# Vector-engine intermediates of a two-part transformer kernel move from SBUF tiles to PSUM banks

## Chip, cores and metric

The kernel runs on one core of one Trainium2 chip. The metric is the device time of one execution in microseconds; the number to predict is the median of several runs.

## What is computed

A 512-token sequence of width 1024 goes through a first block (two layers of feed-forward, mixer, feed-forward and a gated side input) and a second block (four more mixers). What the change touches, in the reference's words:

```python
def swiglu(x, w_in, w_out):
    a, b = jnp.split(x @ w_in, 2, axis=-1)
    return (jax.nn.silu(a) * b) @ w_out

def conformer_conv(glu_in, conv_w, conv_b, g_conv):          # in the mixer of both layers
    a = glu_in[..., :CONV_CH] * jax.nn.sigmoid(glu_in[..., CONV_CH:])
    y = lax.conv_general_dilated(a, conv_w[:, None, :], ..., feature_group_count=CONV_CH) + conv_b
    return jax.nn.silu(rmsnorm(y, g_conv))                    # 31 taps, 512 channels

def hybrid_mixer(u, ...):
    y_attn = forgetting_attention(q, k, v, f_logit) @ w_attn_out   # 8 heads of 64
    y_conv = conformer_conv(z[..., C0:GA0], ...) @ w_conv_out
    merged = jax.nn.sigmoid(z[..., GA0:GC0]) * y_attn + jax.nn.sigmoid(z[..., GC0:]) * y_conv
    return merged @ w_out

def s5_branch(...):                                           # second block
    y = s5_mixer(...); y = y * jax.nn.sigmoid(y @ w_glu + b_glu)
    return (y * jax.nn.silu(z)) @ w_out
```

## The kernel before

All activations are held transposed: 128 channels on the partitions, 512 tokens along the row. A large product is a `Gemm`: one output tile of 128 channels by 512 tokens accumulates in PSUM bank 0 or 1, in turn. Every operand is split into a high part and a low part, and a tile of K = 1024 takes 24 matmuls: high weight times high and low activation for each of 8 chunks (lines 326 and 327), then low weight times high activation (line 335). ScalarE copies the weight's high part out of the DMA buffer (`WH`, line 286), GpSimd subtracts to get the low part (`WL`, line 264, about 2.4 us), and SyncE loads the next weights when `WL` is done. VectorE reads the finished bank (which frees it for the tile after the next) and prepares what follows. When the result is itself an operand of a later product, `split` (lines 407 and 410) makes its halves: a cast into the high tile, then a subtraction into the low tile.

PSUM has eight banks: 0 and 1 for the products' tiles, 2 and 3 for attention scores, 4 and 5 for transposes, 6 and 7 for head values (bank 7 also for the sum of squares at the stage borders).

The places that the change touches:

- **Feed-forward** (`b_vec`, lines 1667 to 1671): the gate product goes through the SBUF tiles `T` and `T2` and is then split into `HH` and `HL`. 88 such tiles.
- **Convolution** (`Conv`, lines 1754 to 1796): 15 of 31 taps per channel group run on VectorE as `y = y + w*x` in the SBUF tile `Y` (line 1763, 176 instructions), the other 16 are multiplied on ScalarE (line 1786) into a ring of four tiles and summed on GpSimd (`YP`, line 1796). `close` (line 1774 and the two after it) adds the two sums. All of this is woven into the products of V, of Q and K, and of the 16 gate tiles (`G`, line 1901): after each product tile every engine's program does its share of the thread. The order is fixed in program text.
- **Attention of the mixer** (`Heads`): also woven into the gate tiles. Pairs of heads go through steps s = 0, 1, ...; PE writes scores of step s, transposes of step s-2 and values (line 1091) of step s-3. VectorE takes maxima (line 1105) and scales (line 1118), and copies a finished pair of heads out of its bank (line 1893) four steps behind. Values of even pairs are in bank 6, of odd pairs in bank 7; PE waits for the copy of the pair before the last.
- **Merging** (`conv_part`, lines 1977 to 1980): eight tiles of K = 512, each with four VectorE instructions: product, sum, cast, subtraction. The product with `w_out` then reads `MH`, `ML`.
- **Gating in the S5 branch** (`glu`, lines 2830 to 2833), **side input** (`flip_p`) and **gated heads** of the second block (`gated_heads`).

The names: `T`, `T2`, `FUN`, `PRE`, `Y`, `YP`, `CA` (convolution input), `G` (gates), `UF`, `ZG`, `PV` (a table of per-channel constants, used as a pointer scalar) are SBUF tiles; `ps` is PSUM.

Of the kernel before, what the change touches and what calls it, by code (L numbers as in the profile page):

```python
# [8 lines left out]
F32 = mybir.dt.float32  # L9
# [3 lines left out]
ALU = mybir.AluOpType  # L13
# [3 lines left out]
P = 128  # L17
# [21 lines left out]
TC = 8  # L39
# [79 lines left out]
class Machine:  # L119


    def __init__(self, nc, ctx):
# [40 lines left out]
        self.ps = ctx.enter_context(nc.psum_tensor("ps", [P, 8, SEQ], F32))  # L163

# [861 lines left out]
class Heads(Thread):  # L1026
# [16 lines left out]

    def block(self, x):

        s, p = divmod(x, 2)
        return 2 * (s // TT) + p, s % TT
# [17 lines left out]
    def tensor(self, e):  # L1065
# [4 lines left out]
        for s in range(self.pairs + lag + 1):  # L1070
# [11 lines left out]
            if s >= lag + 1:  # L1082
                a = 2 * (s - lag - 1)
                e.wait_ge(m.turned.sem, self.b + a + 2)
                h, n = self.block(a)
                if n == 0 and self.h0 + h // 2 > 1:
                    e.wait_ge(m.head_out.sem, self.h0 + h // 2 - 1)
                nb = self.blocks(n)
                for j in range(nb):
                    for p in range(2):  # L1090
                        mm = e.matmul(m.ps[HD * p:HD * p + HD, 6 + h // 2 % 2, n * P:(n + 1) * P], self.v(h + p, n, j),  # L1091
                                      self.buf.PT[:, p, j * P:(j + 1) * P], start=(j == 0), stop=(j == nb - 1))
                        if j == nb - 1:
                            mm.then_inc(m.valued.sem, 1)
# [29 lines left out]
    def heads_out(self, e, s):  # L1124

        m = self.m
        if s < 0 or s % TT != TT - 1:
            return
        c = s // TT
        e.wait_ge(m.valued.sem, self.b + 2 * s + 2)  # L1130
        self.freed = (m.head_out.sem, self.h0 + c + 1)
        self.out(self, e, c, m.ps[:, 6 + c % 2, :])
# [33 lines left out]
    frees = Gemm.frees  # L1166

# [158 lines left out]
def build(nc, out, a):  # L1326
    with ExitStack() as ctx:
# [330 lines left out]
        def ffn(l, w_in, w_out, next_gain, beside, kind=Gemm):  # L1658
# [3 lines left out]
            def pair_of_tiles(first):  # L1662
                tiles = []
                for p in range(2):
                    def b_vec(g, e, i, ps, p=p):
                        v = m.vec
                        e.tensor_tensor(m.T[:], ps, m.R[:], ALU.mult).then_inc(*g.frees())  # L1667
                        e.wait_ge(m.act_out.sem, g.a)
                        e.wait_ge(*v.last)
                        e.tensor_tensor(m.T2[:], m.T[:], m.FUN[:, (g.a0 + p) % 2, :], ALU.mult).then_inc(*v.next())  # L1670
                        g.split(e, at(HH, i * 2 + (first * 2 + p)), at(HL, i * 2 + (first * 2 + p)), m.T2[:])
# [26 lines left out]
        def mixer(l):  # L1698
# [46 lines left out]
            class Conv(Thread):  # L1745
# [7 lines left out]
                def vector(self, e):  # L1753
                    for i in range(CC):
                        y = Y[:, i, :]
                        for j in range(DVE_TAPS):
# [5 lines left out]
                            else:  # L1762
                                e.scalar_tensor_tensor(y, src, wj, y, ALU.mult, ALU.add).then_inc(*v.next())  # L1763
# [130 lines left out]
            att = Heads(m, B, HEADS, q=lambda h, n: head(0, h, slice(n * P, (n + 1) * P)),  # L1894
# [111 lines left out]
        def ple(l):  # L2006
# [5 lines left out]
            def flip_p(c):  # L2012
# [588 lines left out]
        def s5():  # L2601
# [223 lines left out]
            def glu(c):  # L2825
                def f(g, e, i, ps):
# [3 lines left out]
                    e.tensor_tensor(times_(m.T2[:]), UF[:, c, :].rearrange("p (s c) -> p c s", s=TC), times_(ZG[:, c, :]), ALU.mult).then_inc(*v.next())  # L2830
# [50 lines left out]
        def gated_heads(z, high, low):  # L2881

            def f(g, e, c, ps):
                e.wait_ge(*v.last)
                e.tensor_tensor(m.T[:], ps, z[:, c, :], ALU.mult).then_inc(*v.next())
                e.wait_ge(*v.last)
                e.tensor_copy(high[:, c, :], m.T[:]).then_inc(*v.next())
                e.wait_ge(*v.last)
                e.tensor_tensor(low[:, c, :], m.T[:], high[:, c, :].bitcast(F32), ALU.subtract).then_inc(*g.frees())
# [529 lines left out]
```

## Time and profile before

| | us |
|---|---|
| median of 3 runs | 3542.94 (3540.14 to 3543.17) |
| the profiled execution | 3545.91, of which the span 3544.1 |
| TensorE busy in it | 3366.8 (95%) |
| VectorE busy | 2109.5 (60%) |
| GpSimd busy | 1428.6 (40%) |
| ScalarE busy | 1130.3 (32%) |
| mean granted TensorE clock | 0.973 |

The profile gives, for each instruction group, the line of the kernel, the engine, the tiles written and read and its durations. A busy TensorE says little by itself: what counts is whether a product tile takes its shortest period, or longer because a bank was not free or an operand not ready. So the chain that ended last and the waits in order of time are read stage by stage.

### The profile page before, as it was taken

How to read it: one execution, taken by the hardware profiler on the slowest of the kernel's cores; microseconds unless marked ns; L12 is line 12 of the kernel's file. 1: busy time of each engine (PE TensorE's matmuls, PEld its weight loads, DVE VectorE, ACT ScalarE, POOL GpSimd, SP SyncE). 2: the span in 40 equal slices, each digit the busy share in tenths (PEclk: the TensorE clock that was granted, in tenths of full speed). 3: DMA queues.
4: the chain of work that ended last, by engine and by line, in shares of the span. 5: the costliest groups of instructions: out<-in, count | busy, mean ns of one | idle time of the engine just before them, and what ended most of it. 6: DMA issues, size and time to landing. Idle time of an engine off the chain costs nothing.

```text
span 3544.1 us, 43859 instructions
## 1 busy us (share of the span) xinstructions
PE 3366.8 (95%) x16266; PEld 2635.9 (74%) x16266; DVE 2109.5 (60%) x2930; ACT 1130.3 (32%) x1846; POOL 1428.6 (40%) x693
## 2 busy tenths in 40 slices
PE   9999999899999999999998999998989988998998
PEld 6888777678887688887666788876776666776776
DVE  6743399787633576426987864336554648475653
ACT  3222234422222322223343222223324642343332
POOL 4444464344444344445453444443242223322341
PEclk9999999899999999999998999999999989999999
DMA  5333332144423344333212343344642212222221
GB/s 137 95 114 91 95 90 57 45 122 128 134 85 99 95 124 142 91 98 90 71 45 80 116 141 90 94 149 113 211 114 64 60 44 68 60 48 60 85 84 48
DMA packets 632187, 335.01 MB, mean 95 GB/s; under 512 B 97773, under 2 KB 621678, under 8 KB 630478
## 3 DMA queue, kind: packets, MB, share of 16 engines
q1 hardware_dynamic: 607006, 285.75, 28.8%
q10 hardware_dynamic: 23680, 44.32, 3.4%
q0 software_dynamic: 1328, 2.62, 0.2%
q8 instruction: 110, 1.80, 0.2%
q14 instruction: 63, 0.52, 0.0%
HBM read 308.65 MB, written 23.98 MB: 94 GB/s over the span
## 4 chain that ended last, share of the span: by engine, by line
PE 81%; DVE 13%; ACT 3%; issue 2%; ACTq 0%; POOL 0%; DVEq 0%
PE ps L335 24%; PE ps L326 24%; PE ps L327 23%; DVE Y L1763 3%; PE ps L1091 2%; PE ps L1056 1%; PE ps L1080 1%; PE ps L496 1%; DVE T L2832 1%; DVE UL L815 1%; DVE T L824 1%; DVE X L829 0%; PE ps L3204 0%; DVE SS L428 0%; DVE NM L1105 0%
## 5 line engine op out<-in xcount | busy, mean ns | idle before, releaser
L264 POOL TENSOR_TENSOR WL<-RAW,WH 128x1024 fp32r<-128x1024 f32 (+4 forms) x606 | 1321.1, 2182 | 2071.5 <-ACT WH L286 2071.4
L326 PE MATMUL ps<-UH,WH 128*128 128x512 f32 x3056 | 1233.4, 404 | 72.3 <-DVE UL L815 24.8
L327 PE MATMUL ps<-UL,WH 128*128 128x512 f32 x3056 | 1204.6, 394 | 0.0
L286 ACT ACTIVATE WH<-RAW 128x1024 fp32r<-128x1024 f32 (+4 forms) x605 | 571.0, 945 | 1199.8 <-PE ps L335 1169.3
L335 PE MATMUL ps<-UH,WL 128*128 128x512 f32 x3056 | 767.7, 392 | 4.5 <-POOL WL L264 4.5
L326 PEld LDWEIGHTS ps<-UH,WH 128*128 128x128 f32 x3056 | 580.4, 190 | 240.7 <-issue 47.0
L327 PEld LDWEIGHTS ps<-UL,WH 128*128 128x128 f32 x3056 | 580.5, 190 | 125.6 <-issue 7.0
L335 PEld LDWEIGHTS ps<-UH,WL 128*128 128x128 f32 x3056 | 570.9, 188 | 134.3 <-issue 8.6
L326 PE MATMUL ps<-HH,WH 128*128 128x512 f32 x704 | 279.2, 397 | 0.0
L327 PE MATMUL ps<-HL,WH 128*128 128x512 f32 x704 | 276.9, 393 | 0.0
L1763 DVE SCALAR_TENSOR_TENSOR Y<-CA,PV,Y 128x512 f32<-128x512 f32 x176 | 244.8, 1391 | 6.4
L1667 DVE TENSOR_TENSOR T<-ps,R 128x512 f32<-128x512 f32 x88 | 60.8, 691 | 303.3 <-PE ps L335 303.3
L434 DVE SCALAR_TENSOR_TENSOR X<-ps,X 128x512 f32 x48 | 33.2, 692 | 334.5 <-PE ps L335 334.5
L407 DVE CAST HH<-T 128x512 fp32r<-128x512 f32 (+1 forms) x88 | 198.7, 2258 | 5.9 <-DVE T L1670 3.2
L364 DVE TENSOR_TENSOR PRE<-ps,R 128x512 f32<-128x512 f32 x144 | 99.2, 689 | 172.8 <-PE ps L335 168.4
L1676 ACT ACTIVATE FUN<-PRE 128x512 f32<-128x512 f32 x88 | 55.6, 632 | 446.0 <-DVE PRE L364 446.0
L335 PE MATMUL ps<-HH,WL 128*128 128x512 f32 x704 | 185.0, 395 | 0.0
L326 PEld LDWEIGHTS ps<-HH,WH 128*128 128x128 f32 x704 | 132.1, 188 | 33.4
L335 PEld LDWEIGHTS ps<-HH,WL 128*128 128x128 f32 x704 | 132.1, 188 | 32.1
L327 PEld LDWEIGHTS ps<-HL,WH 128*128 128x128 f32 x704 | 132.1, 188 | 30.8
L1148 ACT ACTIVATE S<-ps,NM 128x128 f32<-128x128 f32 (+3 forms) x128 | 66.3, 524 | 126.3 <-DVE NM L1105 121.4
L1080 PE MATMUL ps<-IDENT,S 128*128 128x128 f32 x432 | 72.0, 298 | 23.1 <-ACT PT L1163 11.0
(434 smaller groups left out, 3565.9 us busy)
## 6 DMA issues: line engine op xcount, KB each, us to landing
RAW<-w_ff_in SPq DMA_DIRECT2D x176, 512.0 KB, 3.8
RAW<-w_in SPq DMA_DIRECT2D x72, 512.0 KB, 3.8
RAW<-w_ff_out SPq DMA_DIRECT2D x64, 384.0 KB, 3.4
RAW<-w_ff_out SPq DMA_DIRECT2D x64, 320.0 KB, 3.1
RAW<-d_w_in SPq DMA_DIRECT2D x24, 512.0 KB, 3.8
CM<-cm_dram ACTq DMA_DIRECT2D x8, 1088.0 KB, 10.6
RAW<-b_w_in SPq DMA_DIRECT2D x17, 512.0 KB, 3.7
RAW<-w_out SPq DMA_DIRECT2D x16, 512.0 KB, 3.9
```

The costliest lines, as they stand in the source:

```text
L264: e.tensor_tensor(m.WL[:, s, 0:k, :], m.RAW[:, r, 0:k, :], m.WH[:, s, 0:k, :].bitcast(F32), ALU.subtract).then_inc(m.low_ready.sem, 1)
L286: e.activation(m.WH[:, s, 0:k, :], m.RAW[:, r, 0:k, :], ACT.Copy).then_inc(m.high_ready.sem, 1)
L326: e.matmul(out, m.WH[:, s, c, 0:t.cols], H[:, k0 + c, :], start=(x == 0 and c == 0), stop=False)
L327: e.matmul(out, m.WH[:, s, c, 0:t.cols], L[:, k0 + c, :], start=False, stop=False)
L335: mm = e.matmul(out, m.WL[:, s, c, 0:t.cols], H[:, k0 + c, :], start=False, stop=last)
L364: ins = t.pre(e, i, pre, ps) if t.pre else e.tensor_tensor(pre, ps, m.R[0:t.cols, :], ALU.mult)
L407: e.tensor_copy(high, src).then_inc(*v.next())
L1080: mm = e.transpose(m.ps[:, 4 + a % 2, j * P:(j + 1) * P], self.buf.S[:, a % 4, j * P:(j + 1) * P], m.IDENT[:])
L1091: mm = e.matmul(m.ps[HD * p:HD * p + HD, 6 + h // 2 % 2, n * P:(n + 1) * P], self.v(h + p, n, j), self.buf.PT[:, p, j * P:(j + 1) * P], st ...
L1148: e.activation(B.S[:, c, 0:kk], m.ps[:, 2 + x % 2, 0:kk], ACT.Exp, bias=B.NM[:, c:c + 1], accum_out=B.RS[:, c:c + 1]).then_inc(m.exped.sem, 1)
L1667: e.tensor_tensor(m.T[:], ps, m.R[:], ALU.mult).then_inc(*g.frees())
L1763: e.scalar_tensor_tensor(y, src, wj, y, ALU.mult, ALU.add).then_inc(*v.next())
```

## The change

- `WORK` is PSUM bank 7. The products that are split into halves (feed-forward, merging, S5 gating) are made in place in `WORK` and not in `T`, `T2`; cast and subtraction read it there. `b_vec` gets a wait on VectorE's own last instruction ahead of its first write. In `gated_heads` the values' own bank is used.
- The 15 VectorE taps run in bank 7; the last tap writes `Y` in SBUF.
- Since bank 7 is taken, the mixer's attention uses `OneBankHeads`: all pairs' values are in bank 6, PE waits for the copy of the pair just before, and the copy of a finished pair (but for the last) stands one step earlier in VectorE's program.
- The side input's halves are made straight from its transposed bank, without the copy to `T`; the bank is released after the second instruction.

```diff
+        self.WORK = self.ps[:, 7, :]
...
+class OneBankHeads(Heads):
+    def value_bank(self, c):
+        return 6
+    def wait_values_left(self, e, h, n):
+        if n == 0 and self.h0 + h // 2 > 0:
+            e.wait_ge(self.m.head_out.sem, self.h0 + h // 2)
+    def heads_out(self, e, s):
+        if (s + 1) // TT < self.pairs // TT - 1:
+            s += 1
+        elif s // TT < self.pairs // TT - 1:
+            return
+        super().heads_out(e, s)
...
                     def b_vec(g, e, i, ps, p=p):
-                        e.tensor_tensor(m.T[:], ps, m.R[:], ALU.mult).then_inc(*g.frees())
+                        e.wait_ge(*v.last)
+                        e.tensor_tensor(m.WORK, ps, m.R[:], ALU.mult).then_inc(*g.frees())
...
-                        e.tensor_tensor(m.T2[:], m.T[:], m.FUN[:, (g.a0 + p) % 2, :], ALU.mult).then_inc(*v.next())
-                        g.split(e, at(HH, ...), at(HL, ...), m.T2[:])
+                        e.tensor_tensor(m.WORK, m.WORK, m.FUN[:, (g.a0 + p) % 2, :], ALU.mult).then_inc(*v.next())
+                        g.split(e, at(HH, ...), at(HL, ...), m.WORK)
...
-                        y = Y[:, i, :]
+                        y = m.ps[:, 7, :]
...
-                                e.scalar_tensor_tensor(y, src, wj, y, ALU.mult, ALU.add).then_inc(*v.next())
+                                dst = Y[:, i, :] if j == DVE_TAPS - 1 else y
+                                e.scalar_tensor_tensor(dst, src, wj, y, ALU.mult, ALU.add).then_inc(*v.next())
...
-                    e.tensor_tensor(m.T2[:], ps, G[:, DC + c, :], ALU.mult).then_inc(*g.frees())
+                    e.tensor_tensor(m.WORK, ps, G[:, DC + c, :], ALU.mult).then_inc(*g.frees())
                     e.wait_ge(*v.last)
-                    e.tensor_tensor(m.T2[:], G[:, c, :], m.T2[:], ALU.add).then_inc(*v.next())
-                    g.split(e, MH[:, c, :], ML[:, c, :], m.T2[:])
+                    e.tensor_tensor(m.WORK, G[:, c, :], m.WORK, ALU.add).then_inc(*v.next())
+                    g.split(e, MH[:, c, :], ML[:, c, :], m.WORK)
...
-                    e.tensor_copy(m.T[:], bank).then_inc(*g.frees())
-                    g.split(e, PH[:, c, :], PL[:, c, :], m.T[:])
+                    e.tensor_copy(PH[:, c, :], bank).then_inc(*v.next())
+                    e.wait_ge(*v.last)
+                    e.tensor_tensor(PL[:, c, :], bank, PH[:, c, :].bitcast(F32), ALU.subtract).then_inc(*v.next())
...
-                    e.tensor_tensor(m.T2[:], m.T2[:], g.fun, ALU.mult).then_inc(*v.next())
-                    g.split(e, M2H[:, c, :], M2L[:, c, :], m.T2[:])
+                    e.tensor_tensor(m.WORK, m.WORK, g.fun, ALU.mult).then_inc(*v.next())
+                    g.split(e, M2H[:, c, :], M2L[:, c, :], m.WORK)
```

The instructions of TensorE, ScalarE, GpSimd and SyncE keep their order. On VectorE, in the woven attention of the first layer, before the change (`S` is a scaled block of probabilities, `QKV` takes the heads' values, `NM` a maximum):

```order
L1118 TENSOR_SCALAR S<-S,RINV 128x256 x2
L1901 TENSOR_TENSOR G<-ps,R 128x512
L1763 SCALAR_TENSOR_TENSOR Y<-CA,PV,Y 128x512 x4
L1105 TENSOR_REDUCE NM<-ps 128x1 x2
L1112 RECIPROCAL RINV<-RSUM 128x1 x2
L1118 TENSOR_SCALAR S<-S,RINV 128x384 x2
L1893 COPY QKV<-ps 128x512
L1901 TENSOR_TENSOR G<-ps,R 128x512
```

The same place of VectorE's program after the change:

```order
L1125 TENSOR_SCALAR S<-S,RINV 128x256 x2
L1922 COPY QKV<-ps 128x512
L1930 TENSOR_TENSOR G<-ps,R 128x512
L1792 SCALAR_TENSOR_TENSOR ps<-CA,PV,ps 128x512 x4
L1112 TENSOR_REDUCE NM<-ps 128x1 x2
```

The copy of the pair's values has moved ahead of one gate tile's read-out, four taps and one step of attention; the taps read and write `ps`.

On VectorE in the merging stage, one tile before the change:

```order
L1977 TENSOR_TENSOR T<-ps,G 128x512
L1979 TENSOR_TENSOR T<-G,T 128x512
L407 CAST MH<-T 128x512
L410 TENSOR_TENSOR ML<-T,MH 128x512
```

And after it:

```order
L2006 TENSOR_TENSOR ps<-ps,G 128x512
L2008 TENSOR_TENSOR ps<-G,ps 128x512
L408 CAST MH<-ps 128x512
L411 TENSOR_TENSOR ML<-ps,MH 128x512
```

The count and the order of the four are the same; each now has one operand in PSUM.

## Rows read from the trace of the kernel before

**Rows 1.** The page: busy times, the chain that ended last, the taps' group.

```profile
PE 3366.8 (95%) x16266; PEld 2635.9 (74%) x16266; DVE 2109.5 (60%) x2930; ACT 1130.3 (32%) x1846; POOL 1428.6 (40%) x693
...
PE 81%; DVE 13%; ACT 3%; issue 2%; ACTq 0%; POOL 0%; DVEq 0%
...
L1763 DVE SCALAR_TENSOR_TENSOR Y<-CA,PV,Y 128x512 f32<-128x512 f32 x176 | 244.8, 1391 | 6.4
```

**Rows 2.** Stretches: bounds, length, busy us (instructions) of PE, PEld, DVE, ACT, POOL, clock, DMA.

```profile
187.74:242.14 54.40, 54.40 (x241) 45.05 (x240) 25.99 (x25) 13.22 (x15) 24.82 (x10) 1.00 0.42 132
...
471.31:518.05 46.74, 42.63 (x185) 34.02 (x184) 45.20 (x44) 16.86 (x20) 27.96 (x14) 0.96 0.33 90
518.05:647.69 129.64, 122.10 (x678) 90.98 (x679) 116.63 (x169) 51.41 (x120) 64.52 (x31) 0.97 0.20 53
...
697.89:732.39 34.50, 30.03 (x121) 23.38 (x120) 28.35 (x34) 6.54 (x9) 15.35 (x9) 0.95 0.42 122
2577.58:2628.69 51.11, 42.52 (x171) 32.66 (x170) 40.66 (x38) 12.55 (x16) 16.73 (x7) 0.91 0.42 122
```

**Rows 3.** VectorE by line: count, duration in ns min/median/max, first and last start.

```profile
L1763 DVE SCALAR_TENSOR_TENSOR Y<-CA,PV,Y x176: 750/752/2958, 445.6 to 1853.0; 128x512 f32<-128x512 f32 x176
...
L407 DVE CAST HH<-T x88: 426/2504/2515, 39.9 to 2222.4; 128x512 fp32r<-128x512 f32 x64, 128x512 f32 x24
...
L1667 DVE TENSOR_TENSOR T<-ps,R x88: 676/692/692, 38.4 to 2220.9; 128x512 f32<-128x512 f32 x88
...
L2832 DVE TENSOR_TENSOR T<-T,FUN x8: 2716/2798/2857, 2573.7 to 2620.2; 128x512 f32<-128x512 f32 x8
...
L1893 DVE COPY QKV<-ps x8: 679/682/692, 584.8 to 1867.2; 128x512 f32<-128x512 f32 x8
```

**Rows 4.** Timeline, Q/K and first gate tile: start, length, engine, line, [idle before].

```profile
509.24 2.93 DVE L1763 SCALAR_TENSOR_TENSOR Y<-CA,PV,Y 128x512 f32<-128x512 f32 x2
...
509.26 0.50 PE L326 MATMUL ps<-UH,WH 128*128 128x512 f32 x1 [2.06 <-DVE QKV L1808]
...
516.47 0.60 PE L1832 MATMUL ps<-IDENT,QKV 128*128 128x128 f32 x4
...
526.12 0.49 PE L1056 MATMUL ps<-QKV 64*128 64x128 f32 x4 [2.33 <-DVE V L1878]
```

**Rows 5.** Timeline, the gate tiles of the first layer.

```profile
552.82 0.73 ACT L1786 ACTIVATE T<-CA,PV 128x512 f32<-128x512 f32 x1 [4.19 <-POOL YP L1796]
...
555.47 0.49 PE L1056 MATMUL ps<-QKV 64*128 64x128 f32 x4 [1.82 <-ACT S L1148]
...
619.15 2.70 DVE L1774 TENSOR_TENSOR Y<-Y,YP 128x512 f32<-128x512 f32 x1
...
625.37 0.83 PE L1056 MATMUL ps<-QKV 64*128 64x256 f32 x4 [2.45 <-ACT S L1148]
```

**Rows 6.** Timeline, merging stage of the first layer: first and last VectorE instruction, PE's wait.

```profile
700.96 0.69 DVE L1977 TENSOR_TENSOR T<-ps,G 128x512 f32<-128x512 f32 x1 [1.92 <-issue]
...
729.22 0.69 DVE L410 TENSOR_TENSOR ML<-T,MH 128x512 fp32r<-128x512 f32 x1
...
729.97 0.50 PE L326 MATMUL ps<-MH,WH 128*128 128x512 f32 x1 [1.00 <-DVE ML L410]
```

**Rows 7.** Timeline, S5 gating: one VectorE period and PE's wait behind the last.

```profile
2604.71 0.74 DVE L2875 TENSOR_SCALAR PRE<-ps,PV 128x512 f32<-128x512 f32 x1
2606.16 1.05 DVE L2830 TENSOR_TENSOR T<-UF,ZG 128x512 f32<-128x512 f32 x1 [0.70 <-ACT FUN L2874]
...
2611.21 0.74 DVE L2875 TENSOR_SCALAR PRE<-ps,PV 128x512 f32<-128x512 f32 x1
...
2624.26 0.79 PE L326 MATMUL ps<-M2H,WH 128*128 128x512 f32 x1 [5.69 <-DVE M2L L410]
```

**Rows 8.** Timeline: values of a pair's last step, and VectorE's attention step that goes with it.

```profile
636.73 1.09 PE L1091 MATMUL ps<-PT,V 128*64 128x128 f32 x16
...
638.40 1.01 DVE L1105 TENSOR_REDUCE NM<-ps 128x1 f32<-128x384 f32 x2
```

More of the change, by code:

```diff
@@ L1042, in __init__ @@
         self.t0 = m.tiles
+    def value_bank(self, c):
+        return 6 + c % 2
+    def wait_values_left(self, e, h, n):
+        if n == 0 and self.h0 + h // 2 > 1:
+            e.wait_ge(self.m.head_out.sem, self.h0 + h // 2 - 1)
     def block(self, x):
@@ L1085, in tensor @@
                 h, n = self.block(a)
-                if n == 0 and self.h0 + h // 2 > 1:
-                    e.wait_ge(m.head_out.sem, self.h0 + h // 2 - 1)
+                self.wait_values_left(e, h, n)
                 nb = self.blocks(n)
@@ L1090, in tensor @@
                     for p in range(2):
-                        mm = e.matmul(m.ps[HD * p:HD * p + HD, 6 + h // 2 % 2, n * P:(n + 1) * P], self.v(h + p, n, j),
+                        mm = e.matmul(m.ps[HD * p:HD * p + HD, self.value_bank(h // 2), n * P:(n + 1) * P], self.v(h + p, n, j),
                                       self.buf.PT[:, p, j * P:(j + 1) * P], start=(j == 0), stop=(j == nb - 1))
@@ L1131, in heads_out @@
         self.freed = (m.head_out.sem, self.h0 + c + 1)
-        self.out(self, e, c, m.ps[:, 6 + c % 2, :])
+        self.out(self, e, c, m.ps[:, self.value_bank(c), :])
     def values(self, e, h, n, x):
@@ L1666, in b_vec @@
                         v = m.vec
-                        e.tensor_tensor(m.T[:], ps, m.R[:], ALU.mult).then_inc(*g.frees())
+                        e.wait_ge(*v.last)
+                        e.tensor_tensor(m.WORK, ps, m.R[:], ALU.mult).then_inc(*g.frees())
                         e.wait_ge(m.act_out.sem, g.a)
                         e.wait_ge(*v.last)
-                        e.tensor_tensor(m.T2[:], m.T[:], m.FUN[:, (g.a0 + p) % 2, :], ALU.mult).then_inc(*v.next())
-                        g.split(e, at(HH, i * 2 + (first * 2 + p)), at(HL, i * 2 + (first * 2 + p)), m.T2[:])
+                        e.tensor_tensor(m.WORK, m.WORK, m.FUN[:, (g.a0 + p) % 2, :], ALU.mult).then_inc(*v.next())
+                        g.split(e, at(HH, i * 2 + (first * 2 + p)), at(HL, i * 2 + (first * 2 + p)), m.WORK)
                     for half in range(2):
@@ L1893, in out_heads @@
                 e.tensor_copy(QKV[:, 2 * CC + c, :], ps).then_inc(*g.frees())
-            att = Heads(m, B, HEADS, q=lambda h, n: head(0, h, slice(n * P, (n + 1) * P)),
+            att = OneBankHeads(m, B, HEADS, q=lambda h, n: head(0, h, slice(n * P, (n + 1) * P)),
                         k=lambda h, n: head(CC, h, slice(0, (n + 1) * P)),
@@ L2020, in vec @@
                     e.wait_ge(*v.last)
-                    e.tensor_copy(m.T[:], bank).then_inc(*g.frees())
-                    g.split(e, PH[:, c, :], PL[:, c, :], m.T[:])
+                    e.tensor_copy(PH[:, c, :], bank).then_inc(*v.next())
+                    e.wait_ge(*v.last)
+                    g.si += 1
+                    e.tensor_tensor(PL[:, c, :], bank, PH[:, c, :].bitcast(F32), ALU.subtract).then_inc(*v.next())
+                    e.wait_ge(*v.last)
+                    e.sem_inc(m.splits.sem, 1)
+                    e.sem_inc(*g.frees())
+                    v.last = m.splits.sem, g.s0 + g.si
                 return pe, vec
@@ L2884, in f @@
                 e.wait_ge(*v.last)
-                e.tensor_tensor(m.T[:], ps, z[:, c, :], ALU.mult).then_inc(*v.next())
+                e.tensor_tensor(ps, ps, z[:, c, :], ALU.mult).then_inc(*v.next())
                 e.wait_ge(*v.last)
-                e.tensor_copy(high[:, c, :], m.T[:]).then_inc(*v.next())
+                e.tensor_copy(high[:, c, :], ps).then_inc(*v.next())
                 e.wait_ge(*v.last)
-                e.tensor_tensor(low[:, c, :], m.T[:], high[:, c, :].bitcast(F32), ALU.subtract).then_inc(*g.frees())
+                e.tensor_tensor(low[:, c, :], ps, high[:, c, :].bitcast(F32), ALU.subtract).then_inc(*g.frees())
             return f
```

4 lines of the change are left out of this document (3 added, 1 removed).

## Prediction

> **What bounds the kernel now.** I first read the page's busy times and its chain. TensorE is busy 95% of the span and has 81% of the chain; VectorE has 13% of it [rows 1]. So a faster VectorE pays only where TensorE waits for it, and the next question is where a product tile takes longer than it must. In the feed-forward, ten tiles of K = 1024 take 54.40 us without an idle moment, 5.44 us each, with VectorE busy for half the time [rows 2]. That is the floor of a tile. The feed-forward has most of the tiles, so most of the kernel can't move.
>
> Then I compared other stretches with that floor. In the Q/K stretch (471 to 518) TensorE is busy 42.63 of 46.74 us and VectorE 45.20: VectorE is full there. The gate stretch (518 to 648), the merging (698 to 732) and the S5 gating (2578 to 2629) leave TensorE idle for 7.5, 4.5 and 8.6 us, at a mean clock of 0.97, 0.95 and 0.91 [rows 2]. The second layer repeats the first three.
>
> Last I asked why VectorE is full. Its durations split in two: a tap (line 1763) takes 0.752 us at the median and up to 2.958; the cast into `HH` 0.426 at least and 2.504 at the median; the gate product at line 2832 never less than 2.716; but line 1667, of the same size and with one operand in PSUM, 0.676 to 0.692 over all 88, and the copy out of PSUM at line 1893 0.679 to 0.692 [rows 3]. The long ones read and write SBUF only. They last until a GpSimd instruction ends: GpSimd holds something that VectorE then waits for, and operations with their tensor in PSUM don't need it. That is what the change uses.
>
> The Trainium skill says it so in "SBUF — State Buffer", section "Who interferes with whom": VectorE and GpSimd share a pair of SBUF ports as an exclusive lock, which a VectorE instruction wants with two SBUF inputs or in a two-port mode (cast and copy from SBUF to SBUF). This trace agrees by the durations above; whether a tap with `CA` and the pointer scalar in SBUF and only `y` in PSUM is free of it, no row here shows, and by that rule it is.
>
> **Part 1, feed-forward: 0.** 88 casts go from 2.5 to about 0.69, as line 1893 [rows 3]. VectorE loses some 88 x 1.8 = 160 us of busy time and no path is shorter, since TensorE never waits for it there [rows 2]. The new wait ahead of `b_vec` stands on VectorE's own last instruction, which is done. The cover is large: even doubled, four instructions are under 6 us in two tiles of 5.44.
>
> **Part 2, Q/K stretch: 6.8 us per layer.** Seven tiles take 46.74 us [rows 2]; seven floors are 38.1. Four of them carry a set of four transposes, each at most 0.60 us and, since 0.2 of that overlaps the matmul behind it, about 0.37 [rows 4]: 1.5 to 2.4 us. What is left is 6.3 to 7.2 us; I take 6.8. It consists of waits for a bank that VectorE reads late (2.06 us at 509.26, behind two taps that took 2.93 us together where 1.5 would do [rows 4]) and of the clock, which is at 0.96 of full over the stretch [rows 2]. With taps at 0.75, VectorE's work per tile (one read-out, about two taps, the decay preparation) falls from some 6.5 us to about 4, below 5.44, so a bank is read as soon as it is full and all of this goes.
>
> **Part 3, gate stretch: 6.4 us per layer.** TensorE idles 7.5 us and the clock (0.97 over 129.64 us) costs about 3.4 more [rows 2]. Each wait has another cause. The 2.33 us at 526.12 are for a copy of V that stands behind taps [rows 4]; it goes, and I estimate that half of the lost clock goes with it: 4.0. The 1.82 us at 555.47 are for ScalarE's exponential, but ScalarE was itself held 4.19 us by GpSimd's `YP` and got free at 552.82 [rows 5]. A faster tap only makes GpSimd a little earlier, as it too no longer waits: 1.1. A remainder of 0.9 (7.5 less the three waits named) sits behind four taps: 0.9. The 2.45 us at 625.37 come behind `close`, whose addition at 619.15 took 2.70 us with both tensors in SBUF [rows 5]; it is not changed: 0.4. Sum 6.4. The end of the stretch, from 648 to 666, waits for GpSimd's last sum and stays.
>
> The moved copy of head values: before, PE has written them by 637.8 (636.73 plus 1.09) and VectorE gets to the step at 638.40 [rows 8]. After, it gets there up to 3 us earlier, but its maxima of that step need scores that PE makes just ahead of those values, so it waits at most 1.1 us, three times a layer. Behind it are queued one read-out and the taps, with a tile of slack: 0. PE wants bank 6 again one tile later, some 6 us after the copy: 0.
>
> **Part 4, merging: 5.0 us per layer.** Eight tiles of four instructions run from 700.96 to 729.91, 3.62 us each, and the `w_out` product waits for the last `ML` until 729.97 [rows 6]. After, all four take 0.69 (as line 1667) plus gaps, 2.98: the cast that was 0.43 at best gets slower, those of up to 2.5 [rows 3] go. 8 x 2.98 = 23.9, so `ML` is ready at 724.9. This is still slower than TensorE's 2.72 (half of 5.44), so VectorE stays the bound here.
>
> By the Trainium skill, "VectorE: DVE Perf Modes", section "The TRN2 errata — SBUF-src ops pay a fixed extra latency per instruction", a read from PSUM has a fixed part of 120 cycles against 58, which I estimate at 0.065 us for each; the trace's 0.692 at line 1667, the same as the subtraction of 0.69 from SBUF [rows 3, 6], speaks against it.
>
> **Part 5, S5 gating: 9.5 us, once.** VectorE's period is 6.50 us (2604.71 to 2611.21): 0.74 read-out, 0.70 waiting for ScalarE, 1.05, then 2.8 for line 2832, 0.43 cast, 0.69 subtraction [rows 3, 7]. After: 0.74 + 0.70 + 1.1 + 3 x 0.72 = 4.7, under 5.44. TensorE then runs at its floor: the last tiles, now up to 1.05 late each, give 2.8 in all. The last `M2L` comes 1.8 us sooner after its tile, and of the 5.69 us that PE waits at 2624.26 [rows 7] at least 1.8 goes; the following matmuls run at half clock now (stretch at 0.91 [rows 2]), and the wait left is about 2 us. Worked through: the `M2H` tile starts at 2610.9 and not 2613.66, `M2L` is there at 2616.0, the tile ends at 2618.3 instead of 2628.69. That is 10.4; if a drop of the clock stays, 8.6. I take 9.5.
>
> **Part 6, the rest: +0.5.** `gated_heads` trades a cast of 0.43 for 0.69 at two ends of attention, +0.26 each. The side input saves one instruction that nothing waits for: 0.
>
> **Sum.** 2 x (6.8 + 6.4 + 5.0) + 9.5 - 0.5 = 45.4 us. The profiled execution took 3545.91, which gives 3500.5. The median of the runs is 3.0 lower, so 3497.5; I say 3497.
>
> **The unknown price: an instruction that writes PSUM.** No row of VectorE does so. Nearest is a read from PSUM, 0.69; the cast from SBUF at 0.43 is the lower end and line 2830 with its rearranged operand, 1.05 [rows 3, 7], the upper. A gain below 0.69 is out for two-input forms, since the SBUF ones don't go below it either. I take 0.69. With x us more on each write, the taps lose their gain in proportion to x over 0.64 (mean tap 1.39 [rows 1], less 0.75), the merging loses 16x a layer (two writes, eight tiles) and the gating about 2x, and 14x beyond 0.32. At x = 0.36 the gain falls to about 18 us: 3525.
>
> **Rivals.**
> - *The attention bounds the gate stretch, not VectorE, or the tap stays blocked by its SBUF operands.* For it: the two waits on ScalarE's exponential, GpSimd in ScalarE's way [rows 5]. Against: VectorE is busy 45.2 of 46.7 us in the stretch before. If Parts 2 and 3 give only 0 to 6 a layer, the gain is 19 to 31: 3512 to 3524.
> - *PSUM reads dearer by 0.065*, as the page has it. Three more such reads in each merging tile: 1.6 a layer; 0.2 at the gating's end. 3500.5, inside my range.
> - *PSUM writes dearer*, x = 0.3 to 0.5: 3520 to 3535.
> - *All waits go*, because GpSimd, no longer blocked, frees ScalarE in time and the clock never drops: 2 x (7.2 + 10.9 + 5.5) + 10.4 = 57.6: 3485.
> - *Slower: PSUM writes at 1.4 us and more*, place: taps and merging. By the formula the gain is used up at x = 0.57; at x = 0.8 merging alone costs 2 x 7.8 more and the taps run longer than now: about 3564. Nothing in the rows suggests a price twice that of a read.
> - *The change does nothing*, since all of VectorE's loss is elsewhere: excluded by Part 5, where VectorE's own period sets TensorE's.
>
> **Chances.** Forecast (3490 to 3508, with the page's dearer read in it) 0.58; all waits go 0.15; attention bounds or tap blocked 0.16; dearer writes 0.07; slower 0.04. The range 3480 to 3522 leaves out most of the last two and a little of the third. A measurement of this kernel can tell about 0.2% (7 us) from no change; faster than that: 0.93; within: 0.03; slower: 0.04.
>
> **What would show it.** Taps all near 0.75 and casts near 0.69 whatever GpSimd does; line 2832's successor at 0.69; the Q/K stretch at 40 us for seven tiles; the wait behind `V` gone, the one behind `close` still there; merging at 2.98 a tile; `M2H` tile ending 10 us earlier; VectorE's busy time down by some 280 us. Wrong would be: taps above 0.9, a wait of PE on the copy of head values, or new waits on ScalarE that swallow Part 2.

## The result, and the profile after

The changed kernel takes 3490.36 us (median of 4 runs, 3489.78 to 3494.87), the kernel before 3541.54 beside it (3537.04 to 3543.17): a ratio of 0.9860, 95% interval 0.9843 to 0.9877. It is 51 us faster, where 46 were forecast. The profiled execution took 3489.78, its span 3488.0. Two more sets of the changed kernel gave 3495.15 and 3491.25.

The page, busy times and chain, which answer to [rows 1]:

```profile
PE 3342.4 (96%) x16266; PEld 2624.5 (75%) x16266; DVE 1846.4 (53%) x2926; ACT 1130.7 (32%) x1846; POOL 1384.8 (40%) x693
...
PE 84%; DVE 8%; issue 3%; ACT 3%; POOL 1%; ACTq 0%; DVEq 0%; POOLq 0%
```

VectorE lost 263 us of busy time and its part of the chain fell from 13% to 8%. GpSimd lost 44 us with the same work (27 in its subtractions for the low weights, 17 in its `YP` additions): the two had held each other. Durations on VectorE by line (count, ns min/median/max), against [rows 3]:

```profile
L1792 DVE SCALAR_TENSOR_TENSOR ps<-CA,PV,ps x168: 754/756/757, 440.6 to 1812.1; 128x512 f32<-128x512 f32 x168
L1792 DVE SCALAR_TENSOR_TENSOR Y<-CA,PV,ps x8: 747/748/748, 476.0 to 1812.8; 128x512 f32<-128x512 f32 x8
...
L408 DVE CAST HH<-ps x88: 690/691/693, 34.6 to 2177.8; 128x512 fp32r<-128x512 f32 x64, 128x512 f32 x24
...
L1695 DVE TENSOR_TENSOR ps<-ps,R x88: 698/700/700, 33.1 to 2176.2; 128x512 f32<-128x512 f32 x88
...
L2867 DVE TENSOR_TENSOR ps<-ps,FUN x8: 698/700/700, 2528.3 to 2568.6; 128x512 f32<-128x512 f32 x8
```

Here lies the mechanism: 168 taps within 3 ns of each other, the longest 0.757 us where it was 2.958; 88 casts at 0.69, where the median was 2.50; line 2832's product at 0.70, where it was never under 2.716. A GpSimd instruction runs for at least 0.1 us during 130 of these taps and during all 88 casts, and none of them shows it. (These rows also correct a count given ahead. There are 176 such taps, 22 for each of eight channel groups, four in each layer; with a group's first tap, which is another operation, VectorE has 23 taps of the 31 and ScalarE 8, not 15 and 16.)

The stretches, for [rows 2]: one feed-forward stretch of ten tiles, Q/K, gate, merging, S5 gating. Each holds the same tiles as there, and the columns are the same. The granted clock is 1.00 in all five, where the last four had 0.91 to 0.97.

```profile
182.45:236.85 54.40, 54.40 (x241) 45.06 (x240) 17.36 (x25) 13.21 (x15) 24.00 (x10) 1.00 0.42 132
...
466.05:507.44 41.39, 40.14 (x186) 33.02 (x184) 37.55 (x43) 17.14 (x20) 26.33 (x14) 1.00 0.38 101
507.44:628.97 121.53, 118.81 (x678) 88.66 (x679) 95.75 (x171) 52.30 (x123) 56.51 (x31) 1.00 0.22 57
...
679.18:708.70 29.52, 27.84 (x122) 22.35 (x120) 23.37 (x34) 6.55 (x9) 13.85 (x9) 1.00 0.50 143
2532.22:2573.28 41.06, 39.48 (x172) 31.50 (x171) 28.31 (x37) 12.57 (x16) 16.78 (x7) 1.00 0.51 146
```

Taking the same tiles in both traces (by the starts of their first matmuls), the two spans differ by 56.1 us:

| tiles, by their time in before | before | after | saved |
|---|---|---|---|
| start, to 33 | 32.72 | 27.43 | 5.3 |
| Q/K, 471 to 518 and 1672 to 1719 | 46.74, 46.74 | 41.39, 41.39 | 5.35 + 5.35 |
| gate, 518 to 648 and 1719 to 1849 | 129.64, 129.71 | 121.53, 123.06 | 8.1 + 6.65 |
| behind the gates, to 698 and 1899 | 50.20, 50.70 | 50.21, 49.70 | 0.0 + 1.0 |
| merging, 698 to 732 and 1899 to 1934 | 34.50, 34.55 | 29.52, 29.52 | 5.0 + 5.0 |
| what lies between, mostly feed-forward, 732 to 1672 and 1934 to 2578 | | | 3.7 |
| S5 gating, 2578 to 2629, and the tiles behind | 51.11 | 41.06 | 10.05 + 0.35 |
| gated heads and the rest of the second block | | | 0.3 |

### The profile page after: what moved, and what is told of

Its sections match the earlier page's. It is cut to its first block, busy times and chain, and to the rows that moved or that the text cites. A ratio compares the mean times of both kernels' runs of the same rounds, so it can differ in the third digit from the quotient of the medians.

```text
span 3488.0 us, 43947 instructions
## 1 busy us (share of the span) xinstructions
PE 3342.4 (96%) x16266; PEld 2624.5 (75%) x16266; DVE 1846.4 (53%) x2926; ACT 1130.7 (32%) x1846; POOL 1384.8 (40%) x693
## 4 chain that ended last, share of the span: by engine, by line
PE 84%; DVE 8%; issue 3%; ACT 3%; POOL 1%; ACTq 0%; DVEq 0%; POOLq 0%
PE ps L336 25%; PE ps L327 25%; PE ps L328 25%; PE ps L1098 1%; PE ps L1064 1%; PE ps L1088 1%; POOL WL L265 1%; PE ps L497 1%; DVE UL L816 1%; DVE T L825 1%; POOL YP L1825 0%; PE ps L3239 0%; DVE X L830 0%; DVE SS L429 0%; PE ps L2725 0%
## 5 line engine op out<-in xcount | busy, mean ns | idle before, releaser
L265 POOL TENSOR_TENSOR WL<-RAW,WH 128x1024 fp32r<-128x1024 f32 (+4 forms) x606 | 1294.4, 2137 | 2056.2 <-ACT WH L287 2056.0
L1695 DVE TENSOR_TENSOR ps<-ps,R 128x512 f32<-128x512 f32 x88 | 61.6, 700 | 326.9 <-PE ps L336 326.1
L1792 DVE SCALAR_TENSOR_TENSOR ps<-CA,PV,ps 128x512 f32<-128x512 f32 x168 | 127.0, 756 | 6.1
L1088 PEld LDWEIGHTS ps<-IDENT,S 128*128 128x128 f32 x432 | 49.7, 149 | 36.6 <-issue 15.8
```

The lines of the kernel that those rows point to most:

```text
L265: e.tensor_tensor(m.WL[:, s, 0:k, :], m.RAW[:, r, 0:k, :], m.WH[:, s, 0:k, :].bitcast(F32), ALU.subtract).then_inc(m.low_ready.sem, 1)
L1088: mm = e.transpose(m.ps[:, 4 + a % 2, j * P:(j + 1) * P], self.buf.S[:, a % 4, j * P:(j + 1) * P], m.IDENT[:])
L1695: e.tensor_tensor(m.WORK, ps, m.R[:], ALU.mult).then_inc(*g.frees())
L1792: e.scalar_tensor_tensor(dst, src, wj, y, ALU.mult, ALU.add).then_inc(*v.next())
```

## The experiments

**Which part brings what.** Three kernels, each with one part of the change on the kernel before.

Taps in PSUM and the one bank for head values, the products as before (lines against the changed kernel):

```diff
-                        e.tensor_tensor(m.WORK, ps, m.R[:], ALU.mult).then_inc(*g.frees())
+                        e.tensor_tensor(m.T[:], ps, m.R[:], ALU.mult).then_inc(*g.frees())
...
-                    g.split(e, MH[:, c, :], ML[:, c, :], m.WORK)
+                    g.split(e, MH[:, c, :], ML[:, c, :], m.T2[:])
```

> The kernel before with the convolution's taps in bank 7 and, since they need that bank, the head values of all pairs in bank 6. The products that are split stay in SBUF. Theory (the taps no longer wait for GpSimd): taps at 0.75 us each, the Q/K and gate stretches shorter by 5.4 and 8 us in each layer, so 26 to 27 us in all, 0.9925 of the time before; merging and S5 gating as before. Rival (TensorE's idle time there comes from the chain of attention or from GpSimd holding ScalarE, not from VectorE): taps faster all the same, but the gain under 10 us.

Measured: 3514.52 against 3543.14, ratio 0.9921 (0.9904 to 0.9937). Q/K stretches 41.38 and 41.39, gate 123.10 and 121.62; merging 34.52, S5 gating 51.09 as before.

The products in PSUM, the taps in `Y` and `Heads` with two banks (against the changed kernel too):

```diff
-                        y = m.ps[:, 7, :]
+                        y = Y[:, i, :]
...
-            att = OneBankHeads(m, B, HEADS, ...
+            att = Heads(m, B, HEADS, ...
```

> The change without the taps in PSUM and with two banks for head values: only the products that are split (feed-forward, merging, S5 gating, side input, gated heads) live in PSUM. Theory: merging 5.0 us shorter in each layer, S5 gating 10, nothing in the feed-forward although its 88 casts lose 1.6 us each: 20 us in all, 0.9943. Rival (the feed-forward profits too, since GpSimd makes the low weights sooner): 30 us or more, with tiles under 5.44 us.

Measured: 3520.94 (3510.29 to 3523.11), ratio 0.9929 (0.9909 to 0.9949). Merging 29.52, S5 gating 41.06, to the hundredth the times of after; Q/K and gate as before in the first layer, and 1.9 and 1.7 us longer in the second; and 1.4 us less in the tiles from 732 to 1215, which the taps alone don't give. So "nothing in the feed-forward" was not quite right, and the rival's 30 us are far off.

Only the one bank, with the earlier copy, on the kernel before:

```diff
-            att = Heads(m, B, HEADS, ...
+            att = OneBankHeads(m, B, HEADS, ...
```

> The kernel before with nothing but the head values of all pairs in bank 6 and their copy one step earlier. Theory: no PE wait on that copy, 0 us, within 0.1%. Rival (PE waits for the copy of the pair before, or VectorE waits for PE in the middle of its taps): 3 to 10 us slower.

Measured: 3544.03, ratio 1.0001 (0.9992 to 1.0011, ten runs). Every stretch is within 0.5 us of before. The part that makes room for the rest costs nothing. The two gains, 28.6 and 22.2 us by the medians, add up to the 51.

**Is it GpSimd that VectorE waited for?** In the trace of before, the 80 casts into `HH` that last over 0.9 us all end 0.28 to 0.29 us after a GpSimd instruction does, and the 78 taps of that kind 0.54 to 0.55 us after one. To take the neighbour away: the kernel before, with GpSimd's subtraction for the low weights on 16 of 128 columns. The other columns hold zero, so most of the low weights' part of the products is left out; TensorE's instructions are the same:

```diff
-                    e.tensor_tensor(m.WL[:, s, 0:k, :], m.RAW[:, r, 0:k, :], m.WH[:, s, 0:k, :].bitcast(F32),
+                    e.tensor_tensor(m.WL[:, s, 0:k, 0:16], m.RAW[:, r, 0:k, 0:16], m.WH[:, s, 0:k, 0:16].bitcast(F32),
```

> The kernel before with everything in SBUF as it was, but GpSimd subtracts only 16 of each 128 columns of the low weights (the other columns stay zero; so the low weights' part of the products is mostly left out). TensorE's work is unchanged. Theory (an SBUF operand makes VectorE wait until a running GpSimd instruction ends): casts in the feed-forward fall from 2.25 us in the mean to under 1, line 2832 from 2.8 to about 0.7, taps only meet the convolution's own additions (mean about 1.0); the gain is 35 to 50 us, near the change's 51 without a single operand moved to PSUM. Rival (PSUM operands are faster in themselves, GpSimd has no part in it): casts and taps as long as before, gain under 5 us.

Measured: 3455.12, ratio 0.9755 (0.9739 to 0.9771). VectorE's program is that of before, with all its SBUF operands, and its cast falls from a median of 2.504 us to 0.572:

```profile
L411 DVE CAST HH<-T x88: 426/572/733, 33.7 to 2145.7; 128x512 fp32r<-128x512 f32 x64, 128x512 f32 x24
```

S5 gating takes 40.95, the gate stretch 118.80. The cause is shown, by taking it away from the other side. The gain is much larger than expected, 88 us where 35 to 50 were forecast: it also comes from places that the change leaves alone, such as 6.65 us in the tiles from 732 to 1215 (the change: 1.4) and 3.85 in those to 1268 (0.2). VectorE's other SBUF forms got shorter too (the scaled cast of `X` to `UH` from a median of 2.081 us in after to 0.624 here), but which of them stood on the path there I did not separate. And not all of the 88 is VectorE's: TensorE's waits for `WL` itself, 4.5 us in before and in after, fall to 1.4.

Then the same cut in the changed kernel:

> The changed kernel with GpSimd's low weights cut to 16 of 128 columns, as the short low weights on the kernel before (3455.12 us); leaves out the low weights' part of the products except for those columns. There the stretches of the change were already short (merging 27.78, S5 gating 40.95, Q/K 39.89 us). Theory (all that the change brings is that VectorE does not wait for GpSimd's instructions): with these short it brings next to nothing, only what is left of the wait behind YP in the taps (mean 0.933 us there, 0.756 in after); merging gets slower, since a cast from PSUM takes 0.69 and one from SBUF 0.43 to 0.57, and each write of PSUM 0.008 more: 3451 to 3458. Rival (PSUM operands help by themselves, whatever GpSimd does): the 51 us come off a second time, wholly or by half: 3404 to 3430.

Measured: 3451.72, ratio 0.9745 (0.9731 to 0.9760). The Q/K, gate and S5 stretches take 39.89, 118.77 and 41.06, as without the change; merging takes 29.52 in place of 27.78, and 3215 to 3247 in the second block 32.18 in place of 28.94. Of the last 3.2 us, 2.5 are TensorE's own busy time at a granted clock of 0.84 where it was 1.00. So without GpSimd in the way PSUM operands bring nothing in these stretches, and where all four instructions of a tile are on the path they cost: a cast reads SBUF in 0.43 and PSUM in 0.69. The medians can't tell the cost: the kernel without the change had runs from 3444.71 (the profiled one) to 3459.95, and its median is 3.4 us above this one's. But they leave no room for a second gain of 25 us or more, the rival's.

**How much is the run's own?** The changed kernel twice more, once for the start and once beside the last experiment:

> The changed kernel once more, beside the next ones. The difference of 51.2 us between the medians of before and after has 45 to 46 us in the stretches that the sum names; some 3.5 us lie in the start (14.20 us to the first product tile before, 10.21 after), where the change touches nothing. Theory: the start varies from run to run, so this run gives 3488 to 3495 us with a start anywhere from 10 to 14.2 us. Rival: the change shortens the start; then it is at 10.2 us here again, as in every run that has the change, and at 14.2 in those that don't. Each of the stretches is within 0.3 us of the profiled run of after.

Measured: 3495.15 (3490.92 to 3498.41), start 10.38. This run has the short start too, so alone it can't decide. The two-orders kernel below has the whole change, with a program for the start that is that of after word for word, and its start is the long one. So the rival, that the change shortens the start, is out. Its first product waits, until 14.20, for one VectorE instruction:

```profile
9.95 4.10 DVE L872 SCALAR_TENSOR_TENSOR UL<-X,PV,UH 128x512 fp32r<-128x512 f32 x1 [0.27 <-ACT UH L862]
9.95 1.09 POOL L1558 DMA_DIRECT2D STAGE<-conv_w  x2
...
11.12 2.37 POOL L265 TENSOR_TENSOR WL<-RAW,WH 128x1024 fp32r<-128x1024 f32 x1
```

The same in after:

```profile
9.32 0.75 DVE L872 SCALAR_TENSOR_TENSOR UL<-X,PV,UH 128x512 fp32r<-128x512 f32 x1 [0.27 <-ACT UH L862]
```

It was 4.0 to 4.1 us in before, in the bank-only kernel and in both profiles of the last version below, and 0.75 in all others. In those four it starts at 9.93 to 10.04, between 0.01 us ahead of GpSimd's last two DMA issues and 0.06 behind their start, and ends 0.6 us after GpSimd's first subtraction; in the other ten it starts at 8.52 to 9.93, at least 0.06 us ahead of them. By these rows it is the same hold by GpSimd once more, won or lost by less than 0.1 us of the input's arrival; no run tests it. No line of the change makes the start's 5.3 us. Yet the start went with the kernel wherever one was profiled more than once (short in all three profiles of after, long in both of the two orders), so it isn't shown that it differs between executions of one program, and how much of it the medians hold is open. Another such term is the last stretch. After above, its repeat below, with the same 244 us ahead of the end:

```profile
3244.00:3488.00 244.00, 227.31 (x1052) 176.43 (x1052) 133.83 (x169) 74.33 (x102) 78.86 (x35) 0.95 0.24 72
```

```profile
3252.50:3496.50 244.00, 227.35 (x1045) 176.71 (x1043) 129.35 (x163) 71.85 (x98) 78.87 (x35) 0.94 0.24 72
```

The tiles from 3247 take 297.40 us in one and 302.19 in the other, at one program: the granted clock is at its lower level for 10 or for 20 us near 3400. The gate stretch likewise took 121.53 in one profile of after, 123.16 in the next and 121.57 in a third, and the tiles behind the second layer's gates 49.70, 49.69 and 47.85. Spans of single profiles differ by up to 10 us for such reasons, single stretches by up to 2; Q/K, merging and S5 gating agree within 0.02 in all three.

> The changed kernel, to stand beside the two orders: 3488 to 3496 us.

Measured: 3491.25 (3490.15 to 3493.56).

**What is left in the gate stretch.** In after, VectorE's `close` (three instructions with SBUF operands) still stands ahead of attention's work. First it, then ScalarE's exponential, then PE:

```profile
602.15 2.54 DVE L1803 TENSOR_TENSOR Y<-Y,YP 128x512 f32<-128x512 f32 x1
...
604.73 1.67 DVE L426 TENSOR_TENSOR TURN<-Y 128x512 f32<-128x512 f32 x1
...
607.36 0.37 ACT L1155 ACTIVATE S<-ps,NM 128x128 f32<-128x128 f32 x1 [5.06 <-DVE NM L1112]
...
608.22 0.70 PE L1064 MATMUL ps<-QKV 64*128 64x256 f32 x4 [1.89 <-ACT S L1155]
```

And the last `close` of the layer, which itself waits for GpSimd's sum:

```profile
636.95 1.73 DVE L1803 TENSOR_TENSOR Y<-Y,YP 128x512 f32<-128x512 f32 x1 [4.73 <-POOL YP L1825]
...
640.79 1.58 PE L1088 MATMUL ps<-IDENT,S 128*128 128x128 f32 x8 [4.74 <-DVE S L1125]
...
647.87 0.80 PE L327 MATMUL ps<-UH,WH 128*128 128x512 f32 x1 [0.82 <-DVE QKV L1922]
```

To see what `close` costs, it works on 8 of 512 columns:

```diff
-                    e.tensor_tensor(y, y, YP[:, i, :], ALU.add).then_inc(*v.next())
-                    self.square(e, y)
+                    e.tensor_tensor(y[:, 0:8], y[:, 0:8], YP[:, i, 0:8], ALU.add).then_inc(*v.next())
...
```

> After, with close (line 1803 and its square and running sum, all in SBUF) working on 8 of its 512 columns; leaves out most of the convolution's last addition and of its sum of squares. In the profile of after, TensorE waits 1.89 us at 608.22 behind ScalarE's exponential, 4.74 us at 640.79 behind VectorE's S; ahead of both stands a close whose first instruction lasts 1.7 to 2.7 us. Theory (what is left of the gate stretch's loss comes from the SBUF operations that the change left alone): both waits fall, to under 0.3 us at 608 and to about 1.5 us at 640 (4.74 less the 3.3 us of close), the clock drops for a shorter time behind: 5 to 7 us a layer, 3476 to 3480. Rival (the waits are those of the attention's own chain of scores, exponential, transposes): 0 to 1 us a layer, 3488 to 3490.

Measured: 3484.41, ratio 0.9834 (0.9818 to 0.9850), 11 us below after beside it, 13 by the stretches: 6.5 a layer, as forecast, though the median is above the forecast one, since after itself stood at 3495.15 beside it. Q/K takes 39.89 instead of 41.39, gate 120.08. PE's waits from 500 to 660:

```profile
PE ps L1088 <- DVE S L1125: 3.2, 1, 3.2
PE ps L327 <- DVE QKV L1926: 2.0, 1, 2.0
...
PE ps L1064 <- ACT S L1155: 1.2, 2, 0.8
```

The wait at 608 falls from 1.89 to 0.39, the one at 640 only from 4.74 to 3.2 (1.5 was forecast), and the copy of head values takes over 1.15 of it. So `close` has its price in all three places, though most of the wait at 640 is for what `close` waits for, GpSimd's `YP`. Nor does the cut make the addition short:

```profile
L1803 DVE TENSOR_TENSOR Y<-Y,YP x8: 1206/1632/2173, 503.4 to 1811.6; 128x8 f32<-128x8 f32 x8
```

On 8 columns it still takes 1.2 to 2.2 us: its length is GpSimd's, not its own work's, and this run shows less than the whole price of `close`. That suggests moving it, not shortening it.

**Two orders.** The attention's step ahead of the convolution's in every gate tile:

```diff
-                      [conv_part_of(17), (att, {...})], rhs_ready=u_ready))
+                      [(att, {...}), conv_part_of(17)], rhs_ready=u_ready))
```

> After, with the attention's step put ahead of the convolution's in every tile of the gate stretch, on all engines; nothing is left out. Theory (the 4.74 us at 640.79 are the attention's last S, queued on VectorE behind the last close, which itself waits for GpSimd's YP until 636.95): the attention's last steps no longer stand behind close, the wait goes and with it the drop of the clock at 641 to 653, so 4 to 7 us a layer, 3476 to 3482. Rival (what is moved only changes places: taps and YP run later, the sum of squares is late for the norm's matmul at 651, which then waits as long): within 2 us of after, or slower where TensorE waits for the taps' end.

Measured: 3490.18 (3481.74 to 3491.30), ratio 0.9845, against 3495.15 for after beside it. The gate stretch fell to 118.66 and 118.69, 3 to 4.5 us a layer. Part of it was given back behind, where one new wait is longer than the two that went. Net it is 3.3 and 3.0 us a layer against after beside it, below the 4 to 7 forecast, and the median misses the forecast 3476 to 3482:

```profile
636.92 1.74 DVE L1803 TENSOR_TENSOR Y<-Y,YP 128x512 f32<-128x512 f32 x1 [6.59 <-POOL YP L1825]
...
645.23 0.68 DVE L1922 COPY QKV<-ps 128x512 f32<-128x512 f32 x1
645.96 0.79 PE L327 MATMUL ps<-UH,WH 128*128 128x512 f32 x1 [8.79 <-DVE QKV L1922]
```

The last `close` now blocks the copy of head values instead of `S`. It waits at the head of VectorE's queue. So it is put behind the attention's last work, by three empty steps ahead of it; it then runs where the rest of the convolution's thread is drained:

```diff
+                    for _ in range(3): yield
                     self.close(e, CC - 1)
```

> After, with one thing moved: the convolution's last close (VectorE's addition of YP, square and running sum) stands behind the attention's last step and the four splits of head values, not ahead of them; the other instructions of all engines stand as in after. The 4.74 us that TensorE waits at 640.79 in after, and the half clock from 641 to 653 behind it, come by the reading of the trace from that close, which waits on VectorE for GpSimd's YP until 636.95. Theory: the last S no longer waits, PE's values are written by 637 or so, the copy of head values follows at once and the output product begins some 8 us sooner than at 647.87; the matmul that takes the sum of squares (651.45 in after) then waits up to 2 us for it. 6 to 8 us a layer, 3476 to 3481. Rival: the output product waits instead for the sum of squares or for ScalarE's gates, which run as before: 0 to 2 us a layer, 3488 to 3494.

Measured: 3486.72 (3480.05 to 3487.92), ratio 0.9837 (0.9823 to 0.9852). The 4.74 us are gone; the tiles behind the gate take 14.19 us instead of 18.90, of which 0.6 goes again: 4 a layer, not the 6 to 8 of the theory. The output product begins 4.7 us sooner, not 8, since three of the four splits of head values, with SBUF operands, lie ahead of the copy that it waits for, and GpSimd holds two of their instructions at 1.5 and 1.65 us; it waits 3.10.

Both orders together:

> The move of the last close and the attention's step ahead of the convolution's in each tile, together; nothing is left out. With the attention first, the stretch from 518 to 648 got 4.5 us shorter a layer than in after, but its end moved only from 647.87 to 645.96, since TensorE then waited 8.79 us for the copy of head values, queued on VectorE behind the last close. Theory: without that close in the way, VectorE copies the last head values as soon as they are written (637.2 there), so the output product begins at 638 to 639: 8 to 9 us a layer against after, of which 1 to 2 us go again behind it (waits for the sum of squares): 3474 to 3480, and no better than the last close alone by more than the 1.9 us of the wait at 608. Rival: the rest of the layer takes it back: 3486 to 3491, as with the attention first alone.

Measured: 3485.96 (3478.22 to 3489.56), ratio 0.9833 (0.9817 to 0.9849). Gate stretches 118.67 and 118.68, and TensorE doesn't idle in the 122 us up to 640:

```profile
518.00:640.00 122.00, 122.00 (x715) 91.21 (x713) 99.68 (x175) 55.52 (x128) 54.93 (x31) 1.00 0.20 53
```

By its stretches from 518 to 698 and in the second layer it is 11 us below after, 5.5 a layer where 8 to 9 less 1 to 2 were forecast, and 1.7 a layer below the last close alone; the median misses the forecast 3474 to 3480. The theory had not counted the splits ahead of the copy. But both the long start and 4.8 us of low clock at the end fell into this profile. So it ran again, beside after on the same chip:

> The two orders (the last close later, the attention's step first) once more, beside the changed kernel on the same chip. By the stretches of its first profile it is 11 to 13 us below the changed kernel, in 518 to 698 and in the second layer's part that answers to it; start and last stretch differ by 4 to 5 us from run to run in both. Theory: the median is 9 to 13 us below that of the changed kernel beside it. Rival (the shorter stretches are paid for elsewhere): the medians are within 4 us.

Measured: 3479.55 (3476.69 to 3483.30), ratio 0.9821 (0.9808 to 0.9835), against 3491.25 for after: 11.7 us less, as the stretches say. **This is the fastest version that computes everything, 63 us or 1.8% below the kernel before.** Of its 11 us by the stretches, the last close later gives 7.7 alone and the attention's step first 3.9 alone. What it leaves at this place are the splits of head values, with SBUF operands, in GpSimd's way:

```profile
641.43 1.39 DVE L1943 CAST UH<-QKV 128x512 fp32r<-128x512 f32 x1
642.86 1.64 DVE L1945 TENSOR_TENSOR UL<-QKV,UH 128x512 fp32r<-128x512 f32 x1
644.54 1.37 DVE L1943 CAST UH<-QKV 128x512 fp32r<-128x512 f32 x1
...
647.29 0.79 PE L327 MATMUL ps<-UH,WH 128*128 128x512 f32 x1 [4.85 <-DVE QKV L1922]
```

## The prediction, step by step

Forecast 3497 in 3480 to 3522; it was 3490.4. The mechanism and all large terms held; Parts 1, 2 and 6 had a step wrong, each by less than 4 us in all.

**The tap's freedom** was the open question: by the rule of the Trainium skill ("SBUF — State Buffer", section "Who interferes with whom") a tap with `CA` alone in SBUF should be free. It is: 754 to 757 ns over 168 taps, with `PV` as pointer scalar in SBUF. In this form an accumulator read from PSUM is enough; the last tap, which writes `Y` in SBUF, takes 0.748.

**The price of a PSUM write** was taken as 0.69, with x = 0 more. Measured: 0.700 where [rows 3] have 0.692, so x is 0.008. The rivals with dearer writes fall. So does the dearer PSUM read that the prediction took from the Trainium skill ("VectorE: DVE Perf Modes", section "The TRN2 errata — SBUF-src ops pay a fixed extra latency per instruction"): here the subtraction takes 0.691 from PSUM and 0.69 from SBUF.

**Part 1, feed-forward, said 0: wrong, 3.7 us.** The step "TensorE never waits for it there" came from a stretch of ten tiles without table work. From 818 on, VectorE also turns the S5 tables between feed-forward tiles, and TensorE transposes them. In before, such a tile:

```profile
854.18 2.50 DVE L407 CAST HH<-T 128x512 fp32r<-128x512 f32 x1
...
858.06 0.68 DVE L2226 TENSOR_TENSOR PB<-PB,TURN 128x512 f32<-128x512 f32 x1
858.96 0.69 DVE L364 TENSOR_TENSOR PRE<-ps,R 128x512 f32<-128x512 f32 x1 [0.21 <-DVE PB L2226]
```

The same tile in after:

```profile
830.37 0.69 DVE L408 CAST HH<-ps 128x512 fp32r<-128x512 f32 x1
...
832.90 0.68 DVE L2261 TENSOR_TENSOR PB<-PB,TURN 128x512 f32<-128x512 f32 x1
834.27 0.69 DVE L365 TENSOR_TENSOR PRE<-ps,R 128x512 f32<-128x512 f32 x1 [0.69 <-PE ps L336]
```

The read-out of the next bank waited for the table product behind the long cast; now it waits for PE. This tile, with eight such transposes, takes 6.23 instead of 6.76 us. Five of the eight tiles of this kind get 0.45 to 0.57 us shorter, 2.6 in all; the other three took 6.23 already. The products-only kernel has this gain and the taps-only kernel hasn't. Of the rest, 0.4 lies in two tiles near 1154 and 1221, and 0.6 in one at 2423 whose time isn't steady (14.34, 14.43 and 15.01 in the three profiles of after, 14.94 in before).

**Part 2, Q/K, said 6.8 a layer: 5.35.** The missing 1.5 comes with one wait, the same in both layers. In after:

```profile
501.85 2.70 DVE L1803 TENSOR_TENSOR Y<-Y,YP 128x512 f32<-128x512 f32 x1
...
506.70 0.68 DVE L1839 SCALAR_TENSOR_TENSOR QKV<-ps,R 128x512 f32<-128x512 f32 x1
...
507.44 0.50 PE L327 MATMUL ps<-UH,WH 128*128 128x512 f32 x1 [1.25 <-DVE QKV L1839]
```

"VectorE's work per tile falls to about 4" left out that one tile has a `close` and the decay preparation's contended operations in it. With the small `close` the stretch is at 39.89.

**Part 3, gate, said 6.4: 6.65 and 8.1.** Idle time fell from 7.5 to 2.7 us, so 4.8 of waits went, where 2.33, 1.1, 0.9 and 0.4 had been named. The other part is the clock, of which I gave half: in this profile all of the first layer's loss went (0.97 to 1.00), in the repeat half (123.16 us). The wait behind `close` stayed at 1.89, as said. The moved copy and the one bank cost 0, as said.

**Part 4, merging, said 5.0: 5.0.** The period is 3.01 (2.98 said), and `ML` is still what `w_out` waits for:

```profile
682.25 0.70 DVE L2006 TENSOR_TENSOR ps<-ps,G 128x512 f32<-128x512 f32 x1 [1.92 <-issue]
...
685.26 0.70 DVE L2006 TENSOR_TENSOR ps<-ps,G 128x512 f32<-128x512 f32 x1
...
706.27 0.50 PE L327 MATMUL ps<-MH,WH 128*128 128x512 f32 x1 [1.51 <-DVE ML L411]
```

**Part 5, S5 gating, said 9.5: 10.05**, and 10.4 with the tile behind. 10.4 was worked through for the stretch before I took something off for a drop of the clock, and none came (1.00 in it). VectorE's period is TensorE's 5.44 (2555.17 to 2560.61) and the wait for the last `M2L`, 5.69 before, is 1.57 at 2570.85; about 2 was said.

**Part 6, said to lose 0.5: gained 0.3.** The cast in `gated_heads` was taken at 0.43 before. The one into `ZH`, at the first end, had a mean of 1.11, since GpSimd held it too; the one into `UH`, at the second, a median of 0.43. The first end gained 0.92, the second lost 0.41.

**The sum** left out two things that belong to no part. The start, 5.3 us, is in the two profiles, and no line of the change makes it. The medians differ by 51.2 and the spans less the start by 50.8, which fits medians without it; but the profile of before is also 4.4 us above the median here, so this shows nothing by itself. And the stretch behind the second layer's gates gave 1.0, which is within what it differs by from profile to profile (49.70, 49.69, 47.85). The rival "all waits go" (3485) fell with the waits at 507 and 608; "attention bounds the gate stretch" holds only for what is left.

## What to carry to other kernels

Where one engine may hold up another, read min and median of an instruction's duration: the cast that took 0.43 at best and 2.5 at the median was held by its neighbour, and with its input in PSUM it cost 0.69 always. That paid where VectorE was late, and cost where the form was short and undisturbed. When an engine's work gets shorter by a hundred microseconds "under cover", look at the stretches where it carries a second job before writing 0. And after such a gain the next limit is often an instruction at the head of an in-order queue that waits for another engine, with ready work behind it: moving it, with the attention's step put first, cost no instruction and gave another 12 us.

## What the chip showed that I had not expected

- An instruction with its output in PSUM takes 8 ns more: 0.700 against 0.692 for the products, 0.756 against 0.748 for a tap that reads PSUM.
- The lock works both ways: GpSimd's same 606 subtractions cost it 1294 us instead of 1321.
- Between two profiles of the changed kernel most of the difference is the clock: 4.8 us by whether a drop near the end lasts 10 or 20 us.
- The product in the S5 gating that reads two SBUF tiles and writes PSUM takes 1.110 at the median, where it took 1.05 to 1.11 into SBUF, and 1.345 the one time that it overlapped GpSimd for long (0.83 us). The same instruction in before took 1.347, with as long an overlap. So an output in PSUM alone didn't free it.
